# Feed-forward blocks on 256 tokens: one product of 512 columns for the high weights

## The reference

```python
def _swiglu(h, w_in, w_out):
    g, u = jnp.split(h @ w_in, 2, axis=-1)
    return (jax.nn.silu(g) * u) @ w_out
...
h = h + 0.5 * g2 * _swiglu(_prenorm(h, norm_ffn2[layer], sh2, sc2), ffn2_w_in[layer], ffn2_w_out[layer])
```

## Time and profile before

| | |
|---|---|
| median of 3 runs | 3380.86 us (3376.25 to 3384.05) |
| profiled execution | 3377.81 us, its span 3375.9 us |
| TensorE matmuls busy | 3101.5 us, 92% |
| VectorE, ScalarE busy | 1734.6 us (51%), 1355.1 us (40%) |
| the chain that ended last | TensorE 81%, VectorE 11%, ScalarE 4% |
| clock granted to TensorE, mean | 0.946 of full |

### The profile page before, as it was taken

The page is one execution under the profiler, slowest core; times in us unless marked ns, Lnnn a source line. Parts: engine busy times, 40 slices in busy tenths (PEclk is TensorE's granted clock), DMA queues, the critical chain, the costliest instruction groups (busy, mean ns, idle before and its releaser), DMA issues.

```text
span 3375.9 us, 53187 instructions
## 1 busy us (share of the span) xinstructions
PE 3101.5 (92%) x20138; PEld 2726.3 (81%) x20138; DVE 1734.6 (51%) x2754; ACT 1355.1 (40%) x1942; POOL 0.2 (0%) x4
## 2 busy tenths in 40 slices
PE   6999999889999999999958989899889898998898
PEld 4777778776877878887938989788789887887897
DVE  4333353344333443336376556577555665775555
ACT  3322233323322244224235544354555443545553
POOL 0000000000000000000000000000000000000000
PEclk8999999789999999998988998899989898999899
DMA  7556443014565233323304644355346443553463
GB/s 241 162 165 196 131 158 97 26 38 139 167 184 171 78 97 87 102 83 109 117 0 134 185 143 118 116 153 154 112 133 186 137 118 116 151 155 109 135 187 113
DMA packets 638710, 439.02 MB, mean 130 GB/s; under 512 B 22148, under 2 KB 627168, under 8 KB 638432
## 3 DMA queue, kind: packets, MB, share of 16 engines
q1 hardware_dynamic: 638560, 436.92, 43.8%
HBM read 430.83 MB, written 1.05 MB: 128 GB/s over the span
## 4 chain that ended last, share of the span: by engine, by line
PE 81%; DVE 11%; ACT 4%; issue 3%; SPq 1%; DMA 0%; ACTq 0%; DVEq 0%
PE ps L422 25%; PE ps L423 24%; PE ps L424 23%; DVE wlo L386 3%; PE ps L502 2%; ACT whi L380 1%; DVE normed L1955 1%; PE ps L811 1%; PE ps L509 1%; DVE xl L1949 1%; PE ps L1362 1%; PE ps L820 1%; PE ps L999 1%; PE ps L990 1%; PE ps L1330 1%
## 5 line engine op out<-in xcount | busy, mean ns | idle before, releaser
L422 PE MATMUL ps<-xh,whi 128*128 128x256 f32 (+1 forms) x3744 | 1234.7, 330 | 70.1 <-DVE xl L1949 26.5
L423 PE MATMUL ps<-xl,whi 128*128 128x256 f32 (+1 forms) x3744 | 1212.7, 324 | 0.0
L424 PE MATMUL ps<-xh,wlo 128*128 128x256 f32 (+1 forms) x3744 | 1210.8, 323 | 0.0
L386 DVE TENSOR_TENSOR wlo<-raw,whi 128x1024 fp32r<-128x1024 f32 x732 | 866.6, 1221 | 251.7 <-ACT whi L380 248.9
L380 ACT ACTIVATE whi<-raw 128x1024 fp32r<-128x1024 f32 x732 | 742.9, 1050 | 462.0 <-PE ps L424 414.8
L422 PEld LDWEIGHTS ps<-xh,whi 128*128 128x128 f32 x3744 | 727.2, 194 | 167.1 <-issue 70.4
L424 PEld LDWEIGHTS ps<-xh,wlo 128*128 128x128 f32 x3744 | 728.1, 194 | 51.7
L423 PEld LDWEIGHTS ps<-xl,whi 128*128 128x128 f32 x3744 | 729.1, 195 | 47.3
L422 PE MATMUL ps<-hid_h,whi 128*128 128x512 f32 (+1 forms) x1056 | 360.2, 341 | 9.4 <-DVE wlo L386 9.4
L423 PE MATMUL ps<-hid_l,whi 128*128 128x512 f32 (+1 forms) x1056 | 355.7, 337 | 0.0
L424 PE MATMUL ps<-hid_h,wlo 128*128 128x512 f32 (+1 forms) x1056 | 354.9, 336 | 0.0
(11 more groups left out here) (335 smaller groups left out, 2920.8 us busy)
## 6 DMA issues: line engine op xcount, KB each, us to landing
raw<-ffn_w_in SPq DMA_DIRECT2D x176, 512.0 KB, 4.9
mod_w<-ada_w SPq DMA_DIRECT2D x72, 1024.0 KB, 5.2
raw<-w_in SPq DMA_DIRECT2D x96, 512.0 KB, 3.9
raw<-w_ffn_in SPq DMA_DIRECT2D x88, 512.0 KB, 4.8
raw<-w_gate SPq DMA_DIRECT2D x64, 512.0 KB, 3.9
raw<-ffn_w_out SPq DMA_DIRECT2D x64, 384.0 KB, 4.2
raw<-ffn_w_out SPq DMA_DIRECT2D x64, 320.0 KB, 3.6
raw<-w_branch SPq DMA_DIRECT2D x32, 512.0 KB, 3.8
```

The source lines that it names most:

```text
L386: nc.vector.tensor_tensor(wlo[:, s, h, :], raw[:, s, h, :], whi[:, s, h, :].bitcast(F32), ALU.subtract).then_inc(S("lo_ready"), 1)
L422: nc.tensor.matmul(dst, w_h, x_h, start=start, stop=False)
L423: nc.tensor.matmul(dst, w_h, x_l, start=False, stop=False)
L424: return nc.tensor.matmul(dst, w_l, x_h, start=False, stop=stop)
```

## The change

In the three blocks on 256 tokens the high and the low input lie side by side in one tile (`x_hl`, `hid_hl`; at the addresses that they had). `wide` multiplies `whi` with both at once: 512 columns, which fill a whole PSUM bank, high part left and low part right. `wlo` times the high input is added to the left 256 columns. So a bank holds two halves that have to be added:

- up: VectorE reduces each bank of 2 x 256 to 256 (the gate into `act32`, the other factor into `hid32`); SiLU then works in `act32` in place, and the product is one of two SBUF tiles. New semaphores `gate_sum` and `hid32_ready` order this.
- down: the plain block reduces in the first half and makes two additions in the second; the gated block makes two `scalar_tensor_tensor` in both. Between the two VectorE waits for its own first one (`down_sum`).

The blocks on 512 columns keep `three`.

```diff
@@ -162,14 +162,14 @@
         xh_at = fixed.at
-        xh = fixed("xh", [P, DC, 2 * T], F32R)
-        xl_at = fixed.at
-        xl = fixed("xl", [P, DC, 2 * T], F32R)
+        x_hl = fixed("x_hl", [P, 2, DC, 2 * T], F32R)
+        xl_at = xh_at + 4 * DC * 2 * T
+        xh, xl = x_hl[:, 0, :, :], x_hl[:, 1, :, :]
         overlay = fixed.at
         first = Region(overlay)
-        hid_h = first("hid_h", [P, max(HALVES), 2 * T], F32R)
-        hid_l = first("hid_l", [P, max(HALVES), 2 * T], F32R)
+        hid_hl = first("hid_hl", [P, 2, max(HALVES), 2 * T], F32R)
+        hid_h, hid_l = hid_hl[:, 0, :, :], hid_hl[:, 1, :, :]
         act32 = first("act32", [P, 2, 2 * T])
@@ -423,12 +423,19 @@
+        def wide(bank, w_h, w_l, x_hl, k, start, stop):
+            nc.tensor.matmul(ps[:, bank, :].rearrange("p (a b) -> p a b", a=2), w_h, x_hl[:, :, k, 0:T],
+                             start=start, stop=False)
+            return nc.tensor.matmul(ps[:, bank, 0:T], w_l, x_hl[:, 0, k, 0:T], start=False, stop=stop)
         def half_of(s, h, chunks, width):
-        def pe_blocks(pe, c, i, s, kc, n_tok, x_h, x_l, blocks, width, x_ready=None):
+        def pe_blocks(pe, c, i, s, kc, n_tok, x_h, x_l, blocks, width, x_ready=None, both=None):
@@ -440,9 +447,12 @@
                             x_ready(k)
-                        m = three(ps[:, 2 * s + b, 0:n_tok], w_h[:, j, b * P:(b + 1) * P],
-                                  w_l[:, j, b * P:(b + 1) * P], x_h[:, k, 0:n_tok], x_l[:, k, 0:n_tok],
-                                  k == 0, k == kc - 1)
+                        cols = slice(b * P, (b + 1) * P)
+                        if both is None:
+                            m = three(ps[:, 2 * s + b, 0:n_tok], w_h[:, j, cols], w_l[:, j, cols],
+                                      x_h[:, k, 0:n_tok], x_l[:, k, 0:n_tok], k == 0, k == kc - 1)
+                        else:
+                            m = wide(2 * s + b, w_h[:, j, cols], w_l[:, j, cols], both, k, k == 0, k == kc - 1)
                 m.then_inc(S("mm_done"), 1)
@@ -848,15 +858,18 @@
                                     x_ready(k)
-                                m = three(ps[:, 2 * s + g, 0:n_tok], w_h[:, k, :], w_l[:, k, :],
-                                          xh[:, k, 0:n_tok], xl[:, k, 0:n_tok], k == 0, k == DC - 1)
+                                if n_tok == T:
+                                    m = wide(2 * s + g, w_h[:, k, :], w_l[:, k, :], x_hl, k, k == 0, k == DC - 1)
+                                else:
+                                    m = three(ps[:, 2 * s + g, 0:n_tok], w_h[:, k, :], w_l[:, k, :],
+                                              xh[:, k, 0:n_tok], xl[:, k, 0:n_tok], k == 0, k == DC - 1)
                             m.then_inc(S("mm_done"), 1)
                         pe_blocks(pe, c, i, s, half, n_tok, hid_h, hid_l, 1, P,
-                                  hidden_ready if is_first(i, s) else None)
+                                  hidden_ready if is_first(i, s) else None, hid_hl if n_tok == T else None)
                     for body, total, mod_part in ((up, half // 2, mods[2 * n]), (down, 4, mods[2 * n + 1])):
@@ -1498,11 +1511,18 @@
                     def up(i, s):
-                        unit_done(act, c, i, s, 0)
-                        nc.scalar.activation(act32[:, s, 0:n_tok], ps[:, 2 * s, 0:n_tok], ACT.Silu)\
-                            .then_inc(S("act_ready"), 1)
-                        act.wait_ge(S("evac_done"), 2 * i + (c.units + s + 1 + CREDIT))
+                        if n_tok == T:
+                            act.wait_ge(S("gate_sum"), c.of["gate_sum"] + 2 * i + (hid0 + s + 1))
+                            gate_in = act32[:, s, 0:T]
+                        else:
+                            unit_done(act, c, i, s, 0)
+                            gate_in = ps[:, 2 * s, 0:n_tok]
+                        nc.scalar.activation(act32[:, s, 0:n_tok], gate_in, ACT.Silu).then_inc(S("act_ready"), 1)
+                        if n_tok == T:
+                            act.wait_ge(S("hid32_ready"), c.of["gate_sum"] + 2 * i + (hid0 + s + 1))
+                        else:
+                            act.wait_ge(S("evac_done"), 2 * i + (c.units + s + 1 + CREDIT))
                         nc.scalar.activation(hid_h[:, bass.ds(i * 2 + (hid0 + s), 1), 0:n_tok],
@@ -1510,6 +1530,7 @@
                     c.hidden += half
+                    c.add(gate_sum=half if n_tok == T else 0)
                     for _, pairs, _ in parts(4, mods[2 * n + 1]):
@@ -1966,12 +1987,26 @@
                         a = 2 * i + (a0 + hid0 + s)
-                        dve.wait_ge(S("act_ready"), a + 1)
-                        dve.wait_ge(S("hid_l_ready"), a + 1)
-                        unit_done(dve, c, i, s)
-                        nc.vector.tensor_tensor(hid32[:, s, 0:n_tok], act32[:, s, 0:n_tok],
-                                                ps[:, 2 * s + 1, 0:n_tok], ALU.mult).then_inc(S("evac_done"), 1)
+                        if n_tok == T:
+                            dve.wait_ge(S("hid_l_ready"), a + 1)
+                            unit_done(dve, c, i, s, 0)
+                            nc.vector.tensor_reduce(act32[:, s, 0:T], ps[:, 2 * s, :].rearrange("p (a n) -> p n a", a=2), AX.X, ALU.add)\
+                                .then_inc(S("gate_sum"), 1)
+                            unit_done(dve, c, i, s)
+                            nc.vector.tensor_reduce(hid32[:, s, 0:T], ps[:, 2 * s + 1, :].rearrange("p (a n) -> p n a", a=2),
+                                                    AX.X, ALU.add).then_inc(S("evac_done"), 1)
+                            dve.wait_ge(S("evac_done"), 2 * i + (c.units + s + 1 + CREDIT))
+                            dve.wait_ge(S("act_ready"), a + 1)
+                            nc.vector.tensor_tensor(hid32[:, s, 0:T], hid32[:, s, 0:T], act32[:, s, 0:T], ALU.mult)\
+                                .then_inc(S("hid32_ready"), 1)
+                        else:
+                            dve.wait_ge(S("act_ready"), a + 1)
+                            dve.wait_ge(S("hid_l_ready"), a + 1)
+                            unit_done(dve, c, i, s)
+                            nc.vector.tensor_tensor(hid32[:, s, 0:n_tok], act32[:, s, 0:n_tok],
+                                                    ps[:, 2 * s + 1, 0:n_tok], ALU.mult).then_inc(S("evac_done"), 1)
                         dve.wait_ge(S("hid_h_ready"), a + 1)
@@ -2000,6 +2035,7 @@
                                  before=mod_part and mod_unit(*mod_part))
+                    c.add(down_sum=8 if n_tok == T and (gate or n == 1) else 0)
                 sq_close(1, n_tok)
@@ -2007,12 +2043,15 @@
                     to = bass.ds(i * 2 + (n0 + s), 1)
-                    for j in range(nc_):
-                        sl = slice(j * T, (j + 1) * T)
+                    for j in range(2):
+                        sl = slice(j * T, (j + 1) * T) if nc_ == 2 else slice(0, T)
                         ins = nc.vector.scalar_tensor_tensor(
-                            out=hT[:, to, sl], in0=ps[:, 2 * s:2 * s + 1, sl],
-                            scalar=mod[:, bass.ds(i * 2 + (gate0 + n0 + s), 1), j], in1=hT[:, to, sl],
+                            out=hT[:, to, sl], in0=ps[:, 2 * s:2 * s + 1, j * T:(j + 1) * T],
+                            scalar=mod[:, bass.ds(i * 2 + (gate0 + n0 + s), 1), j if nc_ == 2 else 0], in1=hT[:, to, sl],
                             op0=ALU.mult, op1=ALU.add)
+                        if nc_ == 1 and j == 0:
+                            ins.then_inc(S("down_sum"), 1)
+                            dve.wait_ge(S("down_sum"), 2 * i + (c.of["down_sum"] + n0 + s + 1))
                     ins.then_inc(S("evac_done"), 1)
@@ -2575,11 +2614,14 @@
                     dst = h_out[:, bass.ds(i * 2 + (n0 + s), 1), :]
-                    src = ps[:, 2 * s:2 * s + 1, 0:T]
+                    src, low = ps[:, 2 * s:2 * s + 1, 0:T], ps[:, 2 * s:2 * s + 1, T:2 * T]
                     if n == 0:
-                        ins = nc.vector.tensor_copy(dst, src)
+                        both = ps[:, 2 * s, :].rearrange("p (o a n) -> p o n a", o=1, a=2)
+                        ins = nc.vector.tensor_reduce(dst, both, AX.X, ALU.add)
                     else:
-                        ins = nc.vector.tensor_tensor(dst, src, dst, ALU.add)
+                        nc.vector.tensor_tensor(dst, src, dst, ALU.add).then_inc(S("down_sum"), 1)
+                        dve.wait_ge(S("down_sum"), 2 * i + (c.of["down_sum"] + n0 + s + 1))
+                        ins = nc.vector.tensor_tensor(dst, low, dst, ALU.add)
                     ins.then_inc(S("evac_done"), 1)
```

## The result

The changed kernel took 3397.48 us (median of 5, 3393.23 to 3402.06) against 3380.86 before (median of 5): ratio 1.005, 95% interval 1.0035 to 1.0065, or 12 to 22 us slower. A second comparison of the same two kernels gave 1.0059 (1.0044 to 1.0073). The prediction was 3407 with a range of 3386 to 3448, slower at 0.89. Its profiled execution took 3393.23 us (span 3391.5), 15.4 us more than the one before.

A forecast was written before the change was run, and what follows sets the result against it. TensorE was taken as the bound except in the second down part; a closed loop through VectorE and ScalarE would lengthen the blocks by 9.1, 8.6 and 8.5: +26 us, 3404 profiled, 3407 for the median, range 3386 to 3448.

The forecast's parts named there:

- TensorE's group: TensorE in the 256-token blocks: one 512- and one 256-column matmul take 0.347 us, 0.0133 less than three of 256.
- A sum: VectorE in up units: each reduction of 512 PSUM elements to 256 takes 0.69 us, bounds 0.42 and 1.22.
- rival 1: VectorE's sums read at half rate, 1.22 us each: +68 us in all, 3475; chance 0.15.
- 2 (by results, 0.42): VectorE's sums cost by their results, 0.42 us each: TensorE the bound in up parts, +6 us, 3387; chance 0.05.
- A pair of the first half: First up part: two units through the closed loop take 12.68 us, before 11.52; TensorE no longer the bound.
- A turn of the second half: Second up part: one turn of the closed loop takes 5.68 us; the part changes by -0.2 us.
- A unit of the second down part: Second down part: the addition becomes two with a wait between, 0.48 us more a unit, eight times: +3.9 us.
- The blocks: The three 256-token blocks together: 9.1, 8.6 and 8.5 us longer, +26 us.
- Nothing else in the program moves: Outside the three blocks: buffers lie where they lay and DMA issues are the same, so no time changes there.
- Rival 3: First-half table loads on ScalarE go away: a pair takes 11.35 us, TensorE the bound; +2 us, 3383; chance 0.03.
- Rival 4: Sums and second addition stay out of the path: TensorE saves 6.0 us a block, -18 us, 3363; chance 0.03.
- Rival 5: TensorE's clock falls to 1.2 GHz in the second down part: a unit takes 6.4 us, +36, 3443; chance 0.04.

The follow-up runs named there:

- The second down part alone: The kernel before with only the second down part of each 256-token block made wide: 3386.97 us, ratio 1.0035.
- the delay run: The kernel before plus one unused VectorE reduction ahead of each product of gate and up in the 256-token blocks: 3439.07 us, ratio 1.0189.
- the run without sums: The changed kernel without adding the halves: only the left half of PSUM is read, one operation a unit in down parts; 3365.55 us, ratio 0.9960.

## Why the prediction was right

- **TensorE's group: 0.347 us; it was 0.347 or 0.353.** The term was right for one of two levels and half the saving at the other. In the changed kernel the first down part of the middle block ran at the slow one: a unit took 4.24 us (12 × 0.353), not 4.16; in the gated block 4.16.
- **A sum: 0.69 us; it was 0.684 and 0.683** (66 of each). Rivals 1 (half rate, 1.22) and 2 (by results, 0.42) fell on that row. The Trainium skill ("Advanced Engine Details and Errata", section PSUM Cachelines), named beside rival 1, wants every two consecutive elements contiguous for best throughput and speaks of matmuls. In this read by VectorE it does not show: two values 1 KB apart cost 0.684 us, where the contiguous reduction of as many elements, out of SBUF, cost 0.687.
- **From the gate's sum to the product: 1.38; it was 2510.41 - 2509.09 = 1.32.** The second sum's end to the product costs some 0.04 and not 0.08.
- **A pair of the first half: 12.68; it was 12.53.** From `hid_h` to the copies 0.32 and 1.73, as taken. Up and down part together, from the first product to the next part's: 111.0 us for 105.9, so +5.1 for +4.9.
- **A turn of the second half: 5.68; it was 5.67** (nine in 50.99 us), but this agreement is partly luck. The loop was forecast as the longer one; in fact TensorE had no idle time in the second up part of any block (56.6 of 56.6 us busy in the third window above), and in the middle one it ran at its slow level, where 16 groups take 5.65. In the gated block, at the fast level, a turn was 5.61 and the part took TensorE 55.5 us, against 56.5 in the other two and 57.6 before. Both parts of the second half together, up to the reciprocal: 98.7 for 95.6, +3.2 for the +3.7 that the prediction had for this block.
- **A unit of the second down part: +0.48; it was 4.83 for 4.37.** The second down part alone gave +11.8 us where 8 × 0.48 × 3 is 11.5.
- **The blocks: +26; they took 24.3 and 22.7 more.** The middle and the last block came within 0.3 us (8.3 for 8.6, 8.2 for 8.5); the gated one was 1.3 under (7.8 for 9.1). Two deviations cancel in the middle and the last one, which is luck: a turn of the loop was 0.06 to 0.08 us shorter than worked out, and TensorE's group was at 0.353 in their first down and second up parts. In the gated block these ran at 0.347 and nothing cancelled.
- **"Nothing else in the program moves": this step failed.** No work moved, but the rest took 8.7 and 6.4 us less in the two profiles of after than in the first one of before. 5.1 us of it lie between the middle block and the last, with the clock granted at 1.00 in after where it was 0.89 in before; both kernels repeat this to 0.1 us. 2.7 more (1.4 in the second profile) lie before 780 us, ahead of every change, where one and the same kernel differed by 5.4. So part goes with the changed program, by way of when the clock was low behind its block, and part is luck. The timings fit such a part without proving it: the first comparison (+12 to +22 us) leaves the blocks' 24.3 just outside, the second (+15 to +25) holds the 22.7, and the delay run, +63.7 in the blocks and +63.8 by its ratio, has an interval of 8 us either way. That the time lies inside the forecast owes nothing to this step: without it the blocks' 24.3 give 3405.
- **Rival 3, the table loads go away,** did not come by itself, but could be built with one instruction more. It gave 3379.7 us, 1.7 over before by its ratio and 4.0 in the blocks, for the +2 forecast, with a pair of 11.21 us for the 11.35 worked out. The prediction's working has a slip there: it calls TensorE the bound again at 11.35 us a pair, where its own figure for TensorE is 11.09; by that the first half gains about 1 us in a block and not 3. **Rival 4, the sums out of the path,** was built as the run without sums and gave 3365.6 for 3363 (13.5 under before by its ratio, for 18). **Rival 5**: the clock stayed at 1.00 in the fourth window, with TensorE busy 30.2 of 40.1 us.

So the kernel became slower because TensorE was the path by a small margin only. Without the sums its gain was 15 us, but two sums a unit made a loop through all three engines the longer one, and with that a table load that had been free came to cost 1.3 us a pair; in the second down part, where the loop was the path already, the second addition added its full length.

## What to carry to other kernels

Before work is moved off the busiest engine, write down one turn of the closed loop through the engines that take its results, with every table load and wait in it: the margin to the busiest engine's time is all that the move may cost. When such a loop becomes the path, look first for what was free in it until then; here one instruction ahead of the block gave back most of the loss. And apply a change only where the engine it relieves is the path: the same edit gained 1.5 us in one down part, which is no more than its timing can tell from nothing, and lost 12 us in the other.

## What the runs showed of the hardware

- Groups of a 512- and a 256-column matmul came 0.3467 or 0.3533 us apart at full granted clock, for hundreds of groups on end, and the level of a block changed from one execution of the same kernel to the next. Three matmuls of 256 columns kept 0.360 in every block on 256 tokens that has them.
- The strided sum of two PSUM halves (128x256 from 128x512) took 0.684 us, as a contiguous reduction of 512 out of SBUF does (0.687). The sum of four SBUF tiles (128x256 from 128x1024, the four values 2 KB apart) took 1.99 us, where the contiguous one of 1024 out of PSUM takes 1.219. What makes the second dearer was not looked into.
- One SiLU of one column, ahead of a loop that alternates copies and SiLU, left the loop without its loads of 1.28 us: 2 in a block where there had been 13.
- The same code took from 295.3 to 301.5 us in one stretch that lies ahead of everything changed, with the granted clock at 0.89 or 0.99 in the same windows.
- Behind a block whose own time had changed, the clock was low at other moments: 0.89 or 1.00 in the same 45 us of unchanged code, and 450.8 or 445.7 us for the stretch, each within 0.1 us in two executions of one kernel.
